# Attention two's scores as three rounded products, with the od modulation dealt out anew

## The chip, the cores and the metric

The kernel runs on one core of a Trainium2 chip. The metric is the device time of one execution in microseconds (us), and the time of a kernel is the median of its runs. The engines are TensorE (PE in the rows, PEld its weight loads), VectorE (DVE), ScalarE (ACT), GpSimd (POOL) and SyncE (SP). Each works through its own queue in order, and they meet on semaphores. SyncE and GpSimd here mainly issue DMAs.

## The reference, cut to what matters

Two transformer blocks on x of 256 tokens by 2048 features. The first has causal attention with 8 heads, a conformer convolution and a feed-forward of width 8192. The second has an attention layer ("ev") and a pooling layer ("od"), both with modulation vectors, which are a product of silu(c) with a 2048 x 6144 matrix each:

```
def _modulation(cvec, w, b):
    m = jax.nn.silu(cvec) @ w + b              # shift, scale, gate
...
h  = _rmsnorm(x, pre_g) * (1 + scale) + shift
hc = _rmsnorm(ctx, pre_g) * (1 + scale_c) + shift_c
qA, qB = _split_q(proj[..., :Q_W])             # 8 + 8 heads of 128
kA, vA, kB, vB = _split_kv(...)                # 2 + 2 heads of 128, of x and of ctx
outA = _dense_attention(rope(norm(qA)), [rope(norm(kA)), norm(kA_c)], [vA, vA_c])
outB = _window_attention(rope(qB), rope(kB), vB, kB_c, vB_c, sink)
y = jnp.concatenate([outA, outB], axis=-1) * jax.nn.silu(z)
x = x + gate * _rmsnorm(y @ w_out, post_g)
```

So the second attention has 16 query heads over 256 tokens, each against 512 keys (256 of x, 256 of the context); four query heads share one key head. Everything is float32.

## The kernel before, in words

Products with weights are taken in three rounded parts: a float32 operand is split into a high part, rounded to the type fp32r, and a low part (the rest), and hi x hi, hi x lo and lo x hi are summed. Weights come in blocks of 2048 x 512, by SyncE, a quarter at a time into `raw` (four quarters). A block has 8 steps of 256 rows. Per step ScalarE writes `w_hi` from `raw` (`split_hi`, L552), VectorE writes `w_lo` = raw - w_hi (`split_lo`, L1152), and TensorE multiplies. `w_hi` and `w_lo` have four slots, so ScalarE can split step s+4 once TensorE is done with step s (`step_done`). A quarter of `raw` is loaded again when VectorE is done with it (`split_done`).

Between these splits VectorE does the modulation: `mod_step` (L1192) multiplies 128x1024 of the modulation matrix by a column of silu(c) and adds it to `mod_sum`. Such a multiply-add is called a piece or a half; a vector such as od_shift or od_scale has 32 of them, numbered from 0. The first two (L1189) are plain multiplies. GpSimd loads each piece into one of two halves of `mod_raw` (`load_half`), once the piece two before it is done. After a vector, `turn_parts` transposes and reduces its sum. Where pieces stand is written out by hand. In the feed-forward `ff_mods` counts places p = 8 x block + i (32 blocks of 8 places) and deals pieces out with `spread`; od_shift begins at p = 209, which is in the last group (blocks 24 to 31: four hidden blocks that fill `b_hi`/`b_lo` with relu squared, then four outer ones). In block 28 and on VectorE also adds the block's product to the sum (`last_add`, L1725), ScalarE takes its squares, and VectorE multiplies by the gain and forms products with x (L1736, L1541). SyncE loads two other tensors, `grow` and `table`, once the last hidden part is ready (`hid_ready`, set by `hidden_low`, L1670), and the weights of block 29 and on stand behind them in its queue.

The second attention's projections follow: `evq` (4 blocks, queries), `evkv` (2 blocks, keys and values, each step for x and for the context, so twice as long), `evz` (4 blocks, z). Queries and keys are normed and roped on VectorE, transposed on TensorE and copied out by ScalarE (`q_out`) to `q_T` and `k_T`. While queries are done, the context's columns are scaled, rounded and split in pairs (`ctx_scale`, `ctx_pair`, `ctx_low`).

The heads run beside the z blocks, in 16 slots h = 4i + j (`head_slots` on each engine). TensorE in slot h: scores of head h (L2462), first half of the transposes of head h-1's probabilities (L2437), a z step, the other half, another z step, then v weighed with head h-1's probabilities (L2446). GpSimd stages each query in `q_stage2` and, at every fourth head, v in `v_stage2`. VectorE: maximum (L1874), `late_rope` in slot 0 alone, the normalizing (L1892), two splits, two od_scale pieces. ScalarE: copy of head h-2's output (L990), copy of the first transposed half (L985), exponentials (L1016), a split, the copy of the other half, a split; in slots 4, 8 and 12 first the silu of a z block (L997), which TensorE needs before its first z step of that slot. In slot 2 the keys of the last eight heads are transposed and copied out too.

## Time and profile before

| | |
|---|---|
| median of 3 runs | 1817.17 us (1816.78 to 1817.61) |
| the profiled execution | 1817.8 us, its span 1816.1 us |
| TensorE busy | 1795.7 us (99%) |
| VectorE busy | 1472.4 us (81%) |
| ScalarE busy | 903.3 us (50%) |
| granted TensorE clock | 0.999 |
| DMA | 429.02 MB, 236 GB/s over the span |

TensorE's rows overlap, since matmuls are pipelined: the time that a matmul holds the engine is the distance between two starts, not the length of the row. The same holds to a small part on VectorE and ScalarE, where the next instruction starts up to 0.1 us before the row of the one ahead ends.

### The profile page before, as it was taken

Reading aid. Unit: us, or ns where it says so; the run is one execution under the profiler, and the core shown is the slowest. Engines: PE = TensorE matmul, PEld = TensorE weight load, DVE = VectorE, ACT = ScalarE, POOL = GpSimd, SP = SyncE. Lnnn points to the kernel's source line nnn. Section 1 sums busy time; section 2 is a strip of 40 time slices with the busy share of each in tenths; the row PEclk is TensorE's granted clock in tenths of the full one; section 3 lists DMA queues with packets and bytes.
Section 4 is the critical chain, followed back from the end, with each engine's and each line's share of the span. In section 5 each row is a group of like instructions: output and inputs, shape, how many; then the busy total and the mean of one; then the engine's idle time right before and its main releaser. Section 6 shows DMA issues by size and latency. Waiting matters only on the chain.

```text
span 1816.1 us, 26040 instructions
## 1 busy us (share of the span) xinstructions
PE 1795.7 (99%) x9838; PEld 1553.2 (86%) x9838; DVE 1472.4 (81%) x1712; ACT 903.3 (50%) x1176; POOL 113.5 (6%) x217
## 2 busy tenths in 40 slices
PE   8999999999999999999999999999999999999998
PEld 7899988888888888888888888888888888888986
DVE  6899998878888897889887878765788778897854
ACT  6444566555434433543354557523566546445443
POOL 0000000000000000000000000011111000001000
PEclk9999999999999999999999999999999999999999
DMA  9756447777786787778977966565665784878563
GB/s 324 256 179 192 157 162 291 268 242 265 257 291 228 257 289 233 244 259 295 246 250 267 315 233 235 191 209 164 214 219 191 285 291 130 282 239 283 191 220 105
DMA packets 191304, 429.02 MB, mean 236 GB/s; under 512 B 12512, under 2 KB 12896, under 8 KB 189792
## 3 DMA queue, kind: packets, MB, share of 16 engines
q1 hardware_dynamic: 158560, 323.74, 52.6%
q0 software_dynamic: 27648, 100.68, 16.8%
q10 hardware_dynamic: 4992, 3.16, 0.6%
q8 instruction: 72, 1.18, 0.3%
q14 instruction: 32, 0.26, 0.0%
HBM read 423.33 MB, written 4.21 MB: 235 GB/s over the span
## 4 chain that ended last, share of the span: by engine, by line
PE 94%; DVE 3%; DMA 2%; ACT 1%; issue 1%; SPq 0%; DVEq 0%; ACTq 0%
PE banks L2090 23%; PE banks L2135 14%; PE banks L2137 14%; PE banks L2136 14%; PE banks L2096 12%; PE banks L2081 3%; PE banks L2083 3%; PE banks L2082 3%; PE banks L2446 2%; PE banks L2462 2%; PE banks L2199 1%; PE banks L2437 1%; DVE w_lo L1152 1%; DMA gate_rows<-mod_cols 1%; DMA raw<-in_od_w_out 0%
## 5 line engine op out<-in xcount | busy, mean ns | idle before, releaser
L552 ACT ACTIVATE w_hi<-raw 128x1024 fp32r<-128x1024 f32 x552 | 579.2, 1058 | 648.0 <-PE banks L2137 322.5
L1152 DVE TENSOR_TENSOR w_lo<-raw,w_hi 128x1024 fp32r<-128x1024 f32 x552 | 666.6, 1221 | 229.2 <-ACT w_hi L552 227.0
L2090 PE MATMUL banks<-a_pair,w_hi 128*128 128x512 f32 x1792 | 431.2, 391 | 1.6 <-DVE a_pair L1254 0.9
L2090 PEld LDWEIGHTS banks<-a_pair,w_hi 128*128 128x128 f32 x1792 | 328.4, 188 | 65.2 <-issue 2.2
L2135 PE MATMUL banks<-w_hi,b_hi 128*128 128x512 f32 x808 | 316.2, 391 | 0.2 <-DVE b_lo L1425 0.2
L2137 PE MATMUL banks<-w_hi,b_lo 128*128 128x512 f32 x808 | 314.5, 389 | 0.0
L1192 DVE SCALAR_TENSOR_TENSOR mod_sum<-mod_raw,silu_c,mod_sum 128x1024 f32<-128x1024 f32 x240 | 302.7, 1283 | 14.4 <-DMA mod_raw<-in_od_mod_w 8.1
L2136 PE MATMUL banks<-w_lo,b_hi 128*128 128x512 f32 x808 | 314.4, 389 | 0.0
L2096 PEld LDWEIGHTS banks<-a_pair,w_lo 128*128 128x128 f32 x1792 | 230.2, 191 | 8.8
L2096 PE MATMUL banks<-a_pair,w_lo 128*128 128x256 f32 x1792 | 234.6, 283 | 0.0
L2135 PEld LDWEIGHTS banks<-w_hi,b_hi 128*128 128x128 f32 x808 | 151.7, 188 | 31.9 <-DVE b_lo L1425 0.6
L2137 PEld LDWEIGHTS banks<-w_hi,b_lo 128*128 128x128 f32 x808 | 151.7, 188 | 31.6
L2136 PEld LDWEIGHTS banks<-w_lo,b_hi 128*128 128x128 f32 x808 | 151.7, 188 | 31.3
L2081 PE MATMUL banks<-a_pair,w_hi 128*128 128x256 f32 x512 | 148.4, 290 | 0.0
L2135 PE MATMUL banks<-w_hi,a_pair 128*128 128x512 f32 x368 | 145.1, 394 | 2.0 <-DVE a_pair L1282 0.7
L2083 PE MATMUL banks<-a_pair,w_lo 128*128 128x256 f32 x512 | 144.8, 283 | 0.0
L2082 PE MATMUL banks<-a_pair,w_hi 128*128 128x256 f32 x512 | 144.8, 283 | 0.0
L2137 PE MATMUL banks<-w_hi,a_pair 128*128 128x512 f32 x368 | 143.3, 389 | 0.0
L2136 PE MATMUL banks<-w_lo,a_pair 128*128 128x512 f32 x368 | 143.3, 389 | 0.0
L1368 DVE SCALAR_TENSOR_TENSOR mod_sum<-scratch,cols,mod_sum 128x256 f32<-128x256 f32 x240 | 98.8, 477 | 0.0
L2082 PEld LDWEIGHTS banks<-a_pair,w_hi 128*128 128x128 f32 x512 | 98.2, 192 | 0.3 <-issue 0.2
L2081 PEld LDWEIGHTS banks<-a_pair,w_hi 128*128 128x128 f32 x512 | 98.2, 192 | 0.4 <-ACT scratch L974 0.3
(249 smaller groups left out, 1679.3 us busy)
## 6 DMA issues: line engine op xcount, KB each, us to landing
raw<-in_w_ff SPq DMA_DIRECT2D x128, 1024.0 KB, 6.7
mod_raw<-in_ev_mod_w POOLq DMA_DIRECT2D x96, 512.0 KB, 5.2
mod_raw<-in_od_mod_w POOLq DMA_DIRECT2D x96, 512.0 KB, 5.7
raw<-in_ev_w_in SPq DMA_DIRECT2D x40, 1024.0 KB, 5.7
raw<-in_w_in SPq DMA_DIRECT2D x39, 1024.0 KB, 5.1
raw<-in_od_w_in SPq DMA_DIRECT2D x32, 1024.0 KB, 6.7
raw<-in_w_out SPq DMA_DIRECT2D x16, 1024.0 KB, 6.3
raw<-in_ev_w_out SPq DMA_DIRECT2D x16, 1024.0 KB, 6.8
```

Of the source, the lines that this page charges most:

```text
L552: nc.scalar.activation(w_hi[:, s % SLOTS], raw[:, s // 2, KPS * (s % 2):KPS * (s % 2) + KPS, :], ACT.Copy).then_inc(hi_ready, 1)
L1152: nc.vector.tensor_tensor(w_lo[:, s % SLOTS], raw[:, s // 2, KPS * (s % 2):KPS * (s % 2) + KPS, :], w_hi[:, s % SLOTS].bitcast(F32), ALU.s ...
L1192: nc.vector.scalar_tensor_tensor(s, mod_raw[:, half, :], c, s, ALU.mult, ALU.add).then_inc(mod_acc, 1)
L1368: e = nc.vector.scalar_tensor_tensor(y, src, w, y, ALU.mult, ALU.add)
L2081: nc.tensor.matmul(o, wh, hi[:, k, :], start=first and t == 0 and f % 2 == 0, stop=False, skip_group_check=True)
L2082: nc.tensor.matmul(o, wh, lo[:, k, :], start=False, stop=False, skip_group_check=True)
L2083: last = nc.tensor.matmul(o, wl, hi[:, k, :], start=False, stop=t == KPS - 1, skip_group_check=True)
L2090: e = nc.tensor.matmul(out[:, f, :], w_hi[:, s % SLOTS, t, P * f:P * (f + 1)], rows[:, :, KPS * s + t, :], start=s == 0 and t == 0, stop=F ...
L2096: e = nc.tensor.matmul(out[:, f, T:2 * T], w_lo[:, s % SLOTS, t, P * f:P * (f + 1)], rows[:, 0, KPS * s + t, :], start=False, stop=s == ST ...
L2135: nc.tensor.matmul(o, ah, w_hi[:, slot, t, :], start=s == 0 and t == 0, stop=False, skip_group_check=True)
L2136: nc.tensor.matmul(o, ah, w_lo[:, slot, t, :], start=False, stop=False, skip_group_check=True)
L2137: last = nc.tensor.matmul(o, lo[:, k, P * tt:P * (tt + 1)], w_hi[:, slot, t, :], skip_group_check=True, start=False, stop=s == STEPS - 1 a ...
```

## The change

- The scores of attention two are taken in three rounded products. ScalarE writes the keys rounded (`k_hi`, in `b_hi`) instead of `k_T`, and rounds each query (`round_q`), two heads ahead; VectorE forms the low parts (`keys_low`, `query_low`, into `b_lo`). GpSimd's query copies go.
- ScalarE copies the other half of the transposed probabilities ahead of its split instead of behind it.
- od_shift has 28 of its pieces in the feed-forward, in the place of 16, one in the queries, and three in the first key block, where it is now also turned. od_scale begins there: piece 0 in the first key block, 1 to 8 in the second, two a slot in heads 0 to 7 and one a slot in heads 8 to 14.
- In the last round of the queries the three context pairs stand one place earlier.
- The loops over heads are written out on TensorE, VectorE and in part ScalarE.

```
-            k_T = view(R1, 4, 512)
+            k_hi = [b_hi[:, 4 * i + 2:4 * i + 4, :] for i in range(4)]
+            k_lo = [b_lo[:, 4 * i + 2:4 * i + 4, :] for i in range(4)]
...
GpSimd, heads
-            pool.wait_ge(q_T_ready, 5)
-            stage_q(0, 0)
             first_loads("od_scale", "od", 1, "od_shift")
+            load_mod("od_scale", "od", 1, 1, 5)
+            load_half("od_scale", "od", 1, 5, 0)
+            for h in range(15):
+                if h % 4 == 0:
+                    pool.wait_ge(pv_done, HEAD2 + h + 2)
+                    nc.gpsimd.tensor_copy(v_stage2, v_tok2[:, :, span(h // 4 * HD, HD)]).then_inc(v_staged, 1)
+                for piece in (range(11 + 2 * h, 13 + 2 * h) if h < 8 else range(h + 19, h + 20) if h < 13 else ()):
+                    load_half("od_scale", "od", 1, piece // 2, piece % 2)
...
ScalarE
+            def round_q(h, tile):
+                nc.scalar.activation(b_hi[:, span(tile, 1), :], q_T[:, span(h, 1), :], ACT.Copy).then_inc(q_rounded, 1)
...
                     e.then_inc(exp_done, 1)
+                    if not first or j >= 1:
+                        prob_copy(h - 1, 1)
+                    if j < 2 or not last:
+                        round_q(h + 2, 4 * (i + j // 2) + j % 2)
                     split_hi(ahead[0], [ahead[1]])
                     if first and j == 2:
                         q_out(5)
-                    if not first or j >= 1:
-                        prob_copy(h - 1, 1)
...
VectorE
-                        halves("od_shift", *spread(p, 209, 246, 16))
+                        halves("od_shift", *spread(p, 209, 246, 28))
...
+            def keys_beside(i):
+                if i < 3:
+                    halves("od_shift", 29 + i, 1)
+                elif i < 7:
+                    turn_parts("od_shift", 0, 0, 3, raw_temp, i - 3, 1)
+                else:
+                    halves("od_scale", 0, 1)
...
+            def keys_low(m):
+                dve.wait_ge(q_T_ready, 5 + m)
+                ...
+                e.then_inc(k_low, 1)
+
+            def query_low(h, tile):
+                dve.wait_ge(q_rounded, h + 1)
+                nc.vector.tensor_tensor(b_lo[:, span(tile, 1), :], q_T[:, span(h, 1), :], b_hi[:, span(tile, 1), :].bitcast(F32),
+                                        ALU.subtract).then_inc(q_staged, 1)
...
             def last_keys_beside(i):
+                if i == 4:
+                    keys_low(0)
+                    query_low(0, 0)
+                    query_low(1, 1)
+                halves("od_scale", 1 + i, 1)
...
+                    if first and j == 2:
+                        keys_low(1)
                     split_lo(ahead[0], [ahead[1]])
-                    mod_step("od_scale", 4 * i + j, 0)
+                    if h < 14:
+                        query_low(h + 2, 4 * (i + j // 2) + j % 2)
+                    if h < 15:
+                        halves("od_scale", 2 * h + 9 if h < 8 else h + 17, 1)
                     if j == 3 and not first:
                         z_split(i - 1)
                     split_lo(ahead[0], [ahead[1] + 1])
-                    mod_step("od_scale", 4 * i + j, 1)
+                    if h < 8:
+                        halves("od_scale", 2 * h + 10, 1)
...
TensorE
-                    if first and j in (1, 3):
+                    if first and j in (0, 3):
+                        pe.wait_ge(k_low, 1 + j // 3)
+                    if first and j == 1:
                         pe.wait_ge(acc_free, 2 + ACC["evz"])
-                        pe.wait_ge(q_T_ready, 6 if j == 3 else 5)
                     pe.wait_ge(q_staged, h + 1)
                     for tt in range(TT):
-                        e = nc.tensor.matmul(score2[j % 2][:, 512 * tt:512 * (tt + 1)], q_stage2[:, j % 2, P * tt:P * (tt + 1)],
-                                             k_T[:, span(i, 1), :].rearrange("p a t -> p (a t)"), start=True, stop=True)
+                        out = score2[j % 2][:, 512 * tt:512 * (tt + 1)]
+                        qh = b_hi[:, 4 * i + j % 2, P * tt:P * (tt + 1)]
+                        nc.tensor.matmul(out, qh, k_hi[i].rearrange("p a t -> p (a t)"), start=True, stop=False)
+                        nc.tensor.matmul(out, qh, k_lo[i].rearrange("p a t -> p (a t)"), start=False, stop=False)
+                        e = nc.tensor.matmul(out, b_lo[:, 4 * i + j % 2, P * tt:P * (tt + 1)], k_hi[i].rearrange("p a t -> p (a t)"),
+                                             start=False, stop=True)
```

ScalarE's queue in the slots of heads 1 and 2, before (L552 is a split, L1016 the exponentials, L985 a copy of transposed probabilities, L990 of a head's output, L926 of the keys):

```order
355 L1016 ACTIVATE mod_sum,soft<-banks,soft 128x512 x2
356 L552 ACTIVATE w_hi<-raw 128x1024
357 L985 ACTIVATE scratch<-banks 128x512
358 L552 ACTIVATE w_hi<-raw 128x1024
359 L990 ACTIVATE scratch<-banks 128x256
360 L985 ACTIVATE scratch<-banks 128x512
361 L1016 ACTIVATE mod_sum,soft<-banks,soft 128x512 x2
362 L552 ACTIVATE w_hi<-raw 128x1024
363 L926 ACTIVATE scratch<-banks 128x1024
364 L985 ACTIVATE scratch<-banks 128x512
365 L552 ACTIVATE w_hi<-raw 128x1024
```

And after (L543 is the split, L1020 the exponentials, L989 the probability copy, L926 the rounding of a query, L921 the rounding of the keys):

```order
357 L1020 ACTIVATE mod_sum,soft<-banks,soft 128x512 x2
358 L989 ACTIVATE scratch<-banks 128x512
359 L926 ACTIVATE b_hi<-scratch 128x256
360 L543 ACTIVATE w_hi<-raw 128x1024 x2
361 L994 ACTIVATE scratch<-banks 128x256
362 L989 ACTIVATE scratch<-banks 128x512
363 L1020 ACTIVATE mod_sum,soft<-banks,soft 128x512 x2
364 L989 ACTIVATE scratch<-banks 128x512
365 L926 ACTIVATE b_hi<-scratch 128x256
366 L543 ACTIVATE w_hi<-raw 128x1024
367 L921 ACTIVATE b_hi<-banks 128x512 x2
368 L543 ACTIVATE w_hi<-raw 128x1024
```

The copy of the other half moved from behind the first split to ahead of it, with a rounding between them, and the keys' copy of slot 2 is two copies, now the last thing before the second split.

VectorE's queue from the last split of the key blocks to the reduce of head 1, before (L1874 is the maximum, L1790 to L1795 `late_rope`, L1189 a first piece):

```order
725 L1152 TENSOR_TENSOR w_lo<-raw,w_hi 128x1024
726 L1874 TENSOR_REDUCE soft<-banks 128x2
727 L1880 TENSOR_SCALAR soft<-soft 128x2
...
733 L1892 TENSOR_SCALAR mod_sum<-mod_sum,soft 128x512 x2
734 L1152 TENSOR_TENSOR w_lo<-raw,w_hi 128x1024
735 L1189 TENSOR_SCALAR mod_sum<-mod_raw,silu_c 128x1024
736 L1152 TENSOR_TENSOR w_lo<-raw,w_hi 128x1024
737 L1189 TENSOR_SCALAR mod_sum<-mod_raw,silu_c 128x1024
738 L1874 TENSOR_REDUCE soft<-banks 128x2
```

And after (L1158 is the split, L1198 a piece, L1907 the maximum, L1866 a query's low part):

```order
747 L1158 TENSOR_TENSOR w_lo<-raw,w_hi 128x1024
748 L1198 SCALAR_TENSOR_TENSOR mod_sum<-mod_raw,silu_c,mod_sum 128x1024
749 L1907 TENSOR_REDUCE soft<-banks 128x2
750 L1913 TENSOR_SCALAR soft<-soft 128x2
...
756 L1925 TENSOR_SCALAR mod_sum<-mod_sum,soft 128x512 x2
757 L1158 TENSOR_TENSOR w_lo<-raw,w_hi 128x1024
758 L1866 TENSOR_TENSOR b_lo<-scratch,b_hi 128x256
759 L1198 SCALAR_TENSOR_TENSOR mod_sum<-mod_raw,silu_c,mod_sum 128x1024
760 L1158 TENSOR_TENSOR w_lo<-raw,w_hi 128x1024
761 L1198 SCALAR_TENSOR_TENSOR mod_sum<-mod_raw,silu_c,mod_sum 128x1024
762 L1907 TENSOR_REDUCE soft<-banks 128x2
```

A piece stands ahead of the first maximum, the two of slot 0 are of the longer form, and a subtract is new.

VectorE in the feed-forward, from `hidden_low` of the last hidden block (L1670) to the first `last_add` (L1725), before:

```order
538 L1670 TENSOR_TENSOR b_lo<-scratch,b_hi 128x1024
539 L1152 TENSOR_TENSOR w_lo<-raw,w_hi 128x1024
540 L1192 SCALAR_TENSOR_TENSOR mod_sum<-mod_raw,silu_c,mod_sum 128x1024
541 L1152 TENSOR_TENSOR w_lo<-raw,w_hi 128x1024 x2
542 L1192 SCALAR_TENSOR_TENSOR mod_sum<-mod_raw,silu_c,mod_sum 128x1024
543 L1152 TENSOR_TENSOR w_lo<-raw,w_hi 128x1024 x2
544 L1192 SCALAR_TENSOR_TENSOR mod_sum<-mod_raw,silu_c,mod_sum 128x1024
545 L1152 TENSOR_TENSOR w_lo<-raw,w_hi 128x1024 x2
546 L1725 TENSOR_TENSOR scratch<-scratch,banks 128x512 x2
```

And after, from L1676 to L1731:

```order
546 L1676 TENSOR_TENSOR b_lo<-scratch,b_hi 128x1024
547 L1198 SCALAR_TENSOR_TENSOR mod_sum<-mod_raw,silu_c,mod_sum 128x1024
548 L1158 TENSOR_TENSOR w_lo<-raw,w_hi 128x1024 x2
549 L1198 SCALAR_TENSOR_TENSOR mod_sum<-mod_raw,silu_c,mod_sum 128x1024
550 L1158 TENSOR_TENSOR w_lo<-raw,w_hi 128x1024
551 L1198 SCALAR_TENSOR_TENSOR mod_sum<-mod_raw,silu_c,mod_sum 128x1024
552 L1158 TENSOR_TENSOR w_lo<-raw,w_hi 128x1024
553 L1198 SCALAR_TENSOR_TENSOR mod_sum<-mod_raw,silu_c,mod_sum 128x1024
554 L1158 TENSOR_TENSOR w_lo<-raw,w_hi 128x1024 x2
555 L1198 SCALAR_TENSOR_TENSOR mod_sum<-mod_raw,silu_c,mod_sum 128x1024
556 L1158 TENSOR_TENSOR w_lo<-raw,w_hi 128x1024
557 L1198 SCALAR_TENSOR_TENSOR mod_sum<-mod_raw,silu_c,mod_sum 128x1024
558 L1731 TENSOR_TENSOR scratch<-scratch,banks 128x512 x2
```

Six pieces stand there in the place of three, among the same seven splits.

## Rows read from the trace of the kernel before

**Rows 1.** The page: busy time, share of the span, instructions.
```profile
PE 1795.7 (99%) x9838; PEld 1553.2 (86%) x9838; DVE 1472.4 (81%) x1712; ACT 903.3 (50%) x1176; POOL 113.5 (6%) x217
```

**Rows 2.** Timeline of PE, end of keys, slot 1: start, us, engine, line, op, count.
```profile
1253.37 0.39 PE L2135 MATMUL banks<-w_hi,b_hi 128*128 128x512 f32 x1
...
1255.86 0.39 PE L2137 MATMUL banks<-w_hi,b_lo 128*128 128x512 f32 x1
...
1263.55 1.88 PE L2462 MATMUL banks<-scratch 128*128 128x512 f32 x4
1265.26 0.60 PE L2437 MATMUL banks<-ident,mod_sum 128*128 128x128 f32 x4
...
1268.58 0.60 PE L2437 MATMUL banks<-ident,mod_sum 128*128 128x128 f32 x4
...
1273.64 1.88 PE L2462 MATMUL banks<-scratch 128*128 128x512 f32 x4
```

**Rows 3.** Timeline of DVE, slots 0 and 1.
```profile
1263.81 1.22 DVE L1152 TENSOR_TENSOR w_lo<-raw,w_hi 128x1024 fp32r<-128x1024 f32 x1
1264.94 0.74 DVE L1189 TENSOR_SCALAR mod_sum<-mod_raw,silu_c 128x1024 f32<-128x1024 f32 x1
...
1267.40 1.22 DVE L1874 TENSOR_REDUCE soft<-banks 128x2 f32<-128x1024 f32 x1
```

**Rows 4.** Timeline of ACT, slot 1: in brackets idle time before, and what ended it.
```profile
1268.85 0.69 ACT L1016 ACTIVATE mod_sum<-banks,soft 128x512 f32<-128x512 f32 x1 [2.36 <-DVE soft L1880]
...
1270.19 1.05 ACT L552 ACTIVATE w_hi<-raw 128x1024 fp32r<-128x1024 f32 x1
1271.14 0.59 ACT L985 ACTIVATE scratch<-banks 128x512 f32<-128x512 f32 x1
```

**Rows 5.** Timeline of DVE and ACT, slot 6: a reduce and its exponentials.
```profile
1316.72 1.23 DVE L1874 TENSOR_REDUCE soft<-banks 128x2 f32<-128x1024 f32 x1
...
1318.43 0.69 ACT L1016 ACTIVATE mod_sum<-banks,soft 128x512 f32<-128x512 f32 x1 [0.68 <-DVE soft L1880]
```

**Rows 6.** Groups by line: busy us, mean ns, idle before and releasers.
```profile
L990 ACT ACTIVATE scratch<-banks 128x256 f32<-128x256 f32 (+1 forms) x16 | 6.1, 383 | 8.6 <-PE banks L2446 8.6
L1476 DVE TENSOR_TENSOR b_lo<-scratch,b_hi 128x256 fp32r<-128x256 f32 x8 | 3.2, 422 | 0.4 <-ACT b_hi L793 0.4
```

**Rows 7.** Timeline of ACT, slot 4: the silu of a z block.
```profile
1294.20 1.28 ACT L997 ACT_TABLE_LOAD   x1
1295.50 1.02 ACT L997 ACTIVATE scratch<-banks 128x1024 f32<-128x1024 f32 x1
```

**Rows 8.** Timeline of ACT, feed-forward, last group.
```profile
985.78 1.06 ACT L552 ACTIVATE w_hi<-raw 128x1024 fp32r<-128x1024 f32 x1 [1.66 <-PE banks L2137]
993.24 2.01 ACT L552 ACTIVATE w_hi<-raw 128x1024 fp32r<-128x1024 f32 x2 [6.39 <-DMA raw<-in_w_ff]
```

**Rows 9.** Timeline of DVE, feed-forward, last group.
```profile
982.84 1.22 DVE L1152 TENSOR_TENSOR w_lo<-raw,w_hi 128x1024 fp32r<-128x1024 f32 x1
...
994.33 2.36 DVE L1152 TENSOR_TENSOR w_lo<-raw,w_hi 128x1024 fp32r<-128x1024 f32 x2 [5.03 <-ACT w_hi L552]
...
1000.53 1.28 DVE L1725 TENSOR_TENSOR scratch<-scratch,banks 128x512 f32<-128x512 f32 x2
1003.57 1.22 DVE L1152 TENSOR_TENSOR w_lo<-raw,w_hi 128x1024 fp32r<-128x1024 f32 x1 [1.75 <-ACT w_hi L552]
```

**Rows 10.** Timeline of DVE, around 335 us: pieces close together.
```profile
333.08 1.28 DVE L1192 SCALAR_TENSOR_TENSOR mod_sum<-mod_raw,silu_c,mod_sum 128x1024 f32<-128x1024 f32 x1
334.28 1.21 DVE L1406 TENSOR_TENSOR w_lo<-raw,w_hi 128x1024 fp32r<-128x1024 f32 x1
...
336.84 1.28 DVE L1192 SCALAR_TENSOR_TENSOR mod_sum<-mod_raw,silu_c,mod_sum 128x1024 f32<-128x1024 f32 x1 [1.35 <-DMA mod_raw<-in_ev_mod_w]
...
340.02 1.28 DVE L1192 SCALAR_TENSOR_TENSOR mod_sum<-mod_raw,silu_c,mod_sum 128x1024 f32<-128x1024 f32 x1 [0.76 <-DMA mod_raw<-in_ev_mod_w]
```

**Rows 11.** Waits of PE, 1060 to 1250 us: total, times, longest.
```profile
PE banks L2135 <- DVE b_lo L1323: 0.6, 1, 0.6
```

More of the change, by code:

```diff
@@ L519, in _ @@
             load_mod("od_shift", "od", 0, 1, KT)
-            def stage_q(h, par):
-                if not isinstance(h, int) or h >= 2:
-                    pool.wait_ge(scores, HEAD2 + h - 1)
-                nc.gpsimd.tensor_copy(q_stage2[:, par, :], q_T[:, span(h, 1), :].rearrange("p a t -> p (a t)")).then_inc(q_staged, 1)
-            def head_slots(i, slots):
-                for j in slots:
-                    stage_q(4 * i + j + 1, (j + 1) % 2)
-                    if j == 0:
-                        pool.wait_ge(pv_done, HEAD2 + 4 * i + 2)
-                        nc.gpsimd.tensor_copy(v_stage2, v_tok2[:, :, span(i * HD, HD)]).then_inc(v_staged, 1)
-                    for half in range(2):
-                        load_half("od_scale", "od", 1, 4 * i + j + 1, half)
-            pool.wait_ge(q_T_ready, 5)
-            stage_q(0, 0)
-            first_loads("od_scale", "od", 1, "od_shift")
-            with pool.Fori(0, 3) as i:
-                head_slots(i, range(4))
-            head_slots(3, range(3))
+            first_loads("od_scale", "od", 1, "od_shift")
+            load_mod("od_scale", "od", 1, 1, 5)
[6 more added lines that the diff above has]
+                    load_half("od_scale", "od", 1, piece // 2, piece % 2)
             first_loads("od_gate", "od", 2, "od_scale")
@@ L949, in _ @@
                     q_out(n - 1)
[L950 to L951 removed]
+                split_hi(b + 1, (5, 6))
+                if n == 2:
+                    ctx_pair(pairs[0])
+                split_hi(b + 1, [7])
+                ctx_pair(pairs[n // 2])
                 split_hi(b + 2, (0, 1))
[L953 removed]
+                ctx_pair(pairs[1 + n // 2])
                 split_hi(b + 2, [2])
[L955 removed]
+                if n == 1:
                     ctx_pair(pairs[2])
@@ L1001, in z_round, with head_slots @@
                 nc.scalar.activation(b_hi[:, span(4 * i, FT), :], q_T[:, span(4 * i, FT), :], ACT.Copy).then_inc(z_hi, 1)
-            def head_slots(i, windowed, first=False):
+            def head_slots(i, windowed, first=False, last=False):
                 for j in range(4):
@@ L1032, in _ @@
             head_slots(1, False)
-            with act.Fori(2, 4) as i:
-                head_slots(i, True)
+            head_slots(2, True)
+            head_slots(3, True, last=True)
             prob_copy(15, 0)
@@ L1898, in head_slots @@
                     split_lo(ahead[0], [ahead[1] + 1])
-                    mod_step("od_scale", 4 * i + j, 1)
+                    if h < 8:
+                        halves("od_scale", 2 * h + 10, 1)
             head_slots(0, False, True)
             head_slots(1, False)
-            with dve.Fori(2, 4) as i:
+            for i in range(2, 4):
                 head_slots(i, True)
@@ L2479, in _ @@
             head_slots(0, True)
-            with pe.Fori(1, 4) as i:
+            for i in range(1, 4):
                 head_slots(i)
```

45 lines of the change are left out of this document (25 added, 20 removed).

## The prediction

> **What bounds the kernel now.** I read the busy table of the page first: TensorE is busy 1795.7 of 1816.1 us [rows 1], so only what shortens its own work, or makes it wait, can move the time. Then I read its timeline through the second attention. Each head there is one "slot" on TensorE: the scores, four transposes, a step of the z product (24 rounded matmuls), four transposes, another such step, and the product with v. Slot 1 runs from 1263.55 to 1273.64, 10.09 us, with nothing missing between the parts [rows 2]. VectorE and ScalarE serve it from behind: the softmax, and the splitting of raw weights into w_hi (ScalarE) and w_lo (VectorE), some steps ahead. VectorE also works through the modulation in "pieces", one 128x1024 multiply-add each, for which it waits for nobody as a rule. So the question is what the change takes from TensorE, and whether the two helpers keep their lead with the work dealt out anew.
>
> **What TensorE saves.** A head's scores are two products of 128x512, and they hold TensorE from 1263.55 to 1265.26, 1.71 us [rows 2]. The new form is six rounded matmuls of 512 columns with the pattern of the weight products; twelve of those start between 1253.37 and 1255.86 (eleven intervals), 0.226 us each [rows 2]. Six are 1.36 us. Saved: 0.35 x 16 heads = 5.7 us. The end of the q blocks gets one context pair earlier, which can take away the one wait of 0.6 us that stands there [rows 11]. With nothing else the kernel would stand at 1817.8 - 6.3 = 1811.5 by its own profiled execution.
>
> **What the attention gives back.** I follow the slots with the intervals of the rows: split 1.13 (1263.81 to 1264.94) [rows 3], piece 1.20 (333.08 to 334.28) [rows 10], reduce to exponentials 1.45 [rows 3, 4] or 1.71 [rows 5], exponentials 1.34 and probability copy about 0.5 [rows 4]. The new rounding of a query on ScalarE has the size of its 128x256 copies, 0.38 [rows 6], of which about 0.1 overlaps its neighbour (estimate, as piece and split overlap); the new subtract on VectorE is that of a 128x256 row, 0.42 [rows 6], 0.36 without overlap. Bounds for both: not below 0.2 and not above the 0.5 to 0.6 of the 128x512 copy [rows 4]; the chosen values are those of rows of the same size.
> Slot 0 and 1. Before, the last key block ended on a split, and slot 0 had the two first pieces, plain multiplies of 0.74, 0.66 without overlap [rows 3]. Now piece 8 stands ahead of the first reduce (+1.20), slot 0 has two full pieces (+1.1) and a query subtract (+0.36). Head 0's probabilities, ready by 1263.81 [rows 3], come at 1265.0; TensorE, 0.35 earlier than before, asks at 1263.55 - 0.35 + 1.36 = 1264.55: a wait of 0.5. The reduce of head 1 goes from 1267.40 to 1270.05. Behind it in ScalarE's queue are the exponentials and only then the second copy of head 0's probabilities, which ends at 1270.05 + 1.45 + 1.34 + 0.5 = 1273.4. Before, that copy ended at 1271.73 [rows 4] and TensorE used it at 1268.58 + 3.31 = 1271.89 [rows 2]: no room at all. Now it asks at 1271.7: a wait of 1.7.
> Slots 2 and 3. VectorE now must subtract the keys of heads 8 to 15 before TensorE may start scores 3, and ScalarE writes their rounded form only after exponentials, copy, rounding and a split. After the copy at 1273.4 ScalarE rounds and splits till 1274.7, VectorE then does split, subtract, piece, split, piece (5.0) and begins the reduce of head 2 at 1279.75: 1279.8 + 1.45 + 1.34 + 0.5 + 0.3 + 1.0 + 1.0 (two key copies) = 1285.4, subtract 1.25, so 1286.65. TensorE began slot 2 at 1275.2 and with the key transposes (0.87) needs 10.6 for it, so it asks at 1285.8: 1.0 of wait, and 0.65 more at v, since VectorE comes late to head 3.
> From slot 3 on a loop closes: ScalarE's split stands behind copy and rounding, and VectorE's rest of the slot behind that split. 1.71 + 1.34 + 0.5 + 0.3 + 1.05 = 4.9, then split 1.14, subtract 0.36, piece, split, piece (3.54): 9.9 us a slot against TensorE's 9.73. VectorE doesn't regain its lead in heads 3 to 7. In heads 8 to 14 one piece is gone but the band's add is there: 9.6, just enough. So at each head 4, 8 and 12 the z-silu, with its table load, comes late. Before, it ran from 1295.50 to about 1296.5 [rows 7] for a TensorE that needs it some 2.07 us into the slot (1265.26 + 0.36 after 1263.55), 0.2 later. Now TensorE asks 0.35 earlier and ScalarE is about a microsecond later: 1.1, 0.8, 0.9, and 1.1 at v in slot 8, behind the z_split of VectorE (1.14). Sum of waits 7.7, less 5.7 saved: the attention ends about 2.0 us later than before. With 1.45 in all slots it is +1.1, with 1.71 in all +2.9; the outer ends are -5.7 (no wait) and about +6 (each wait half as large again). The other moves of this stretch I put at nothing: GpSimd's query copies go, its four v copies now wait for a v product with two loads queued behind each, but such a load is wanted some 8 us after that product and loads took 5 to 6.9 in pairs [rows 10]; the first key block loses VectorE work while TensorE waits for nothing there; the unrolled loops hold the same instructions. Bounds 0 and 0.5 each.
> The Trainium skill (ScalarE: Activation LUTs, What ACT_TABLE_LOAD costs) counts 1.28 us for the load and 1.38 more of drain at each switch. Here the load starts at 1294.20 and the silu at 1295.50 [rows 7], so only the 1.28 shows, and I use that; by the page each of the three heads would be 1.4 later still, which by an estimate is +4.
>
> **What the feed-forward gives.** Between places 209 and 246 (944 to about 1043 us) 28 pieces stand where 16 stood: 12 x 1.20 = 14.4 us more on VectorE, and their loads. Nobody on TensorE waits in this stretch before. Two things make it tight. First the loads: mod_raw has two buffers, so piece n+2 is loaded only once n is done. Where pieces follow each other closely, starts two apart are 6.94 us apart (333.08 to 340.02, with VectorE waiting 0.76 for the DMA [rows 10]): 3.5 us a piece at best. 28 pieces in 37 places are 3.6 us a piece on average, but they stand three in a row at 2.7, so most triples wait 1 to 2 us, in VectorE's queue, ahead of splits and of hidden_low.
> Second the entry to the last outer blocks. SP holds the weights of the second outer block behind two other loads, and these behind hidden_low, which ends at 982.84 + a little (the row of that start is the split behind it [rows 9]). ScalarE waited 6.39 us for these weights, till 993.24, and the split on VectorE started at 994.33 [rows 8, 9] and was done at 995.5. TensorE needs it at 985.6 (step 3 done [rows 8]) + 4 x 2.72 = 996.5. So 1.0 us of room. Now one piece (1.20) and a wait of 1 to 1.5 come ahead of hidden_low: everything moves 2.5 us, a wait of about 1.7. Then, up to the add that ends the block (1000.53 before), there are three pieces for one, the start is 2.5 later, one more load wait of 1.5: about 1007. The add releases ScalarE's squares and then the split of step 4, which on VectorE starts 3.04 later (1003.57 - 1000.53 [rows 9]): 1010.1, done 1011.3, against a need at 996.5 + 1.7 + 4 x 2.72 = 1009.1: 2.3 more. Each of the two blocks after that costs VectorE 8 x 1.13 + 6 x 1.20 + 2.6 (gained and products) + 1.3 (add) + 1.75 (idle behind the add [rows 9]) = 21.9 and about a microsecond of load waits, against 21.8 of TensorE: about 1.2 each. Sum +6.4. If two pieces need 6.0 us instead of 6.9, the same count gives +1.7 to +4; if they need 8, as they may when the weights catch up after 984, +10 to +13. Bounds 0 and 14.
>
> **Sum.** 1817.8 + 2.0 + 6.4 - 0.6 = 1825.6; the median of the runs is 0.6 below the profiled one, so 1825.0.
>
> **Rivals.**
> 1. The saving arrives. VectorE is busy only 81% [rows 1], and the waits above are each about a microsecond, at the edge. If rounding and reordering cost nothing visible: 1817.2 - 5.7 - 0.6, with 0 to 1 from the feed-forward: 1811 to 1812. Against it: the margins of 0.2 us at the v product and the silu in slots 1 and 4 [rows 2, 4, 7]. Chance 0.15.
> 2. The feed-forward hides its pieces (loads land within 4.5 us there), the attention goes as worked out: 1817.2 + 2.0 - 0.6 + 1 = about 1819.6, no change that can be told. Chance 0.2.
> 3. The loads get slower under 28 pieces, so VectorE is late throughout: +12 instead of +6.4, 1831. For it: the loads of this stretch compete with 1 MB of weights each 5.4 us. Chance 0.12.
> 4. The six products don't run at 0.226 but at the 0.43 of a pass of today's scores (1.71 / 4), since both operands change their source: 2.6 us a head, +0.9 x 16 = 14, 1831 to 1840. Against it: all weight products read b_hi as here [rows 2]. Chance 0.03.
> The forecast itself, 1821 to 1829, has 0.5.
>
> **How the numbers follow.** A difference under 0.2% (3.6 us) can't be told from none. Faster, below 1813.6: nearly all of rival 1, 0.15 with a little from elsewhere 0.16. Same, to 1820.8: rival 2 and the lower edge of the forecast, 0.25. Slower: 0.59. The range 1812.5 to 1832 leaves out half of rival 1 and the upper part of 3 and 4.
>
> **What would show it.** Right: the scores take 1.36 us a head; TensorE waits in slot 1 for a probability copy on ScalarE, in slot 3 for b_lo of the keys, in slots 4, 8 and 12 for the silu; VectorE's pieces wait for DMA between 950 and 1045; the first split of the second last outer block is later than 996.5, and TensorE waits for w_lo in three or four places there. Wrong: no TensorE wait between 940 and 1065, or slots of 9.7 us throughout, or a wait at a place where I have none, such as the first key block, where VectorE loses work.

## The result: 1830.0 us, slower by 0.7%

The changed kernel takes 1830.02 us (median of 6 runs, 1826.42 to 1831.24); the kernel before, run beside it, 1817.15 (1816.78 to 1818.3). The ratio is 1.0068, 95% interval 1.0055 to 1.0081. The profiled run of the changed kernel is its fastest, 1826.42 with a span of 1824.7: 8.6 over the span before. So its trace shows two thirds of the loss of the median.

The page of the changed kernel. TensorE is busy as long as in [rows 1], and the span is 8.6 longer:

```profile
span 1824.7 us, 25842 instructions
PE 1795.2 (98%) x9870; PEld 1560.7 (86%) x9870; DVE 1479.4 (81%) x1732; ACT 903.9 (50%) x1194; POOL 105.4 (6%) x201
```

What TensorE waited for, whole span (line and releaser: us in total, times, longest):

```profile
PE banks L2174 <- DVE w_lo L1158: 6.5, 4, 2.8
...
PE banks L2238 <- DVE ln_rstd L1252: 2.7, 2, 2.0
PE banks L2485 <- issue: 2.3, 2, 1.5
...
PE banks L2120 <- ACT scratch L1001: 0.7, 1, 0.7
PE banks L2504 <- DVE b_lo L1859: 0.6, 1, 0.6
PE banks L2476 <- DVE mod_sum L1925: 0.5, 1, 0.5
```

The first line is the feed-forward, the second the norm products behind it (the wait of 2.0 at 1077.14 was 1.15 before), the last four are the attention. To see what each stage costs, I lay TensorE's landmarks of both traces side by side (start of the same work, us):

| landmark | before | after | later by |
|---|---|---|---|
| end of the feed-forward's products (first `ones` product) | 1062.24 | 1071.19 | 8.95 |
| first norm product | 1067.35 | 1077.14 | 9.79 |
| scores of head 0 | 1256.09 | 1264.96 | 8.87 |
| v product of head 15 | 1422.23 | 1431.93 | 9.70 |
| end of the span | 1816.1 | 1824.7 | 8.6 |

So the feed-forward costs 8.95 and its tail 0.85 at the norm; the q blocks give back 0.9; the attention, whose slots are 5.2 shorter in all without their waits, loses 0.83; and 1.1 comes back behind it (0.6 of it a wait for w_lo at 1748 that the kernel before had and this one doesn't).

**The feed-forward.** TensorE's waits there:

```profile
999.14 0.47 PE L2174 MATMUL banks<-w_hi,b_hi 128*128 128x512 f32 x1 [2.75 <-DVE w_lo L1158]
...
1013.11 0.47 PE L2174 MATMUL banks<-w_hi,b_hi 128*128 128x512 f32 x1 [2.80 <-DVE w_lo L1158]
1013.42 0.40 PE L2175 MATMUL banks<-w_lo,b_hi 128*128 128x512 f32 x1
...
1014.74 0.63 PE L2174 MATMUL banks<-w_hi,b_hi 128*128 128x512 f32 x1
1015.17 0.63 PE L2175 MATMUL banks<-w_lo,b_hi 128*128 128x512 f32 x1
```

Two waits of 2.8 where the forecast had 1.7 and 2.3; two of 0.45 follow. Together 6.45, but the stage is 8.95 longer. The last two rows hold the rest: 1.6 us after the second wait the matmuls start every 0.43 us instead of every 0.23. The windows (busy time and count of PE, granted clock, DMA share, GB/s) say why:

```profile
1012.00:1016.00 4.00, 2.89 (x9) 0.79 0.70 274
1016.00:1020.00 4.00, 4.00 (x15) 0.78 0.63 186
1020.00:1024.00 4.00, 4.00 (x19) 1.00 1.04 406
```

The clock was at its lower level (1.2 GHz) for part of these eight microseconds. Eight matmuls, from 1014.33 on, start 0.43 apart in place of 0.23: 1.6 us more for the same work (1.7 by the windows, whose mean is 0.785). Each of the four waits costs 0.24 beyond its bracket, 1.0 in all: from 996.01, the last start ahead of the first wait, to 999.45, the second start behind it, are 3.44 us, where two intervals of 0.23 and the 2.75 make 3.20. Against that the outer blocks began 0.24 earlier than before (974.47 against 974.71).

Why w_lo was late shows on VectorE and ScalarE in the stretch of [rows 8, 9] (in brackets the idle time before and what ended it):

```profile
983.78 1.23 DVE L1676 TENSOR_TENSOR b_lo<-scratch,b_hi 128x1024 fp32r<-128x1024 f32 x1 [0.94 <-ACT b_hi L838]
...
994.27 1.28 DVE L1198 SCALAR_TENSOR_TENSOR mod_sum<-mod_raw,silu_c,mod_sum 128x1024 f32<-128x1024 f32 x1 [3.46 <-DMA mod_raw<-in_od_mod_w]
997.77 1.23 DVE L1158 TENSOR_TENSOR w_lo<-raw,w_hi 128x1024 fp32r<-128x1024 f32 x1 [2.22 <-ACT w_hi L543]
...
1007.51 1.28 DVE L1198 SCALAR_TENSOR_TENSOR mod_sum<-mod_raw,silu_c,mod_sum 128x1024 f32<-128x1024 f32 x1 [2.14 <-DMA mod_raw<-in_od_mod_w]
1008.71 1.28 DVE L1731 TENSOR_TENSOR scratch<-scratch,banks 128x512 f32<-128x512 f32 x2
1011.74 1.23 DVE L1158 TENSOR_TENSOR w_lo<-raw,w_hi 128x1024 fp32r<-128x1024 f32 x1 [1.75 <-ACT w_hi L543]
```

```profile
996.68 2.00 ACT L543 ACTIVATE w_hi<-raw 128x1024 fp32r<-128x1024 f32 x2 [10.07 <-DMA raw<-in_w_ff]
```

The weights of the second outer block come at 996.68 instead of 993.24, 3.4 later, and the first split starts at 997.77 instead of 994.33. Where the 3.4 us come from shows on SyncE's queue (start times, and the time from the first issue of these weights to ScalarE's first split of them):

| kernel | `hidden_low` | weights issued | first w_hi | issue to w_hi |
|---|---|---|---|---|
| before | 981.70 | 984.12 | 993.24 | 9.12 |
| changed | 983.78 | 986.21 | 996.68 | 10.47 |

So 2.1 us come from VectorE's queue ahead of `hidden_low`, and 1.35 from weights that take longer to land. The wait of 3.46 for the piece at 994.27 costs TensorE nothing by itself: the split behind it still waits 2.22 for the weights. The wait of 2.14 for the piece at 1007.51 does cost: it stands right ahead of the add. That add, forecast for "about 1007", begins at 1008.71, and the split of step 4 is at 1011.74, not 1010.1.

**The attention.** TensorE in slots 1 to 4, and ScalarE where it made TensorE wait:

```profile
1272.15 0.40 PE L2504 MATMUL banks<-b_hi 128*128 128x512 f32 x1
...
1274.16 0.66 PE L2476 MATMUL banks<-ident,mod_sum 128*128 128x128 f32 x4 [0.46 <-DVE mod_sum L1925]
...
1282.51 1.97 PE L2485 MATMUL banks<-scratch 128*128 128x256 f32 x8 [1.50 <-issue]
1284.12 0.59 PE L2504 MATMUL banks<-b_hi 128*128 128x512 f32 x1
...
1295.68 0.50 PE L2504 MATMUL banks<-b_hi 128*128 128x512 f32 x1 [0.60 <-DVE b_lo L1859]
...
1308.52 0.39 PE L2120 MATMUL banks<-a_pair,w_hi 128*128 128x256 f32 x1 [0.69 <-ACT scratch L1001]
```

```profile
1281.72 0.20 ACT L1020 ACTIVATION_READ_ACCUMULATOR mod_sum<-banks,soft 128x1 f32 x1
1281.81 0.59 ACT L989 ACTIVATE scratch<-banks 128x512 f32<-128x512 f32 x1
...
1306.14 1.28 ACT L1001 ACT_TABLE_LOAD   x1
1307.44 1.02 ACT L1001 ACTIVATE scratch<-banks 128x1024 f32<-128x1024 f32 x1
```

"issue" at 1282.51 is a wait that no semaphore record names; ScalarE's row at 1281.81 names it: the copy ends at 1282.40, and v starts 0.11 later. The places are those of the forecast: the probabilities and their second copy in slot 1, the keys' b_lo at scores 3, the silu at slot 4, and v in slot 8 (0.83); the silus of slots 8 and 12 delay their first z step by only 0.2 and 0.4. The slots of heads 0 to 14, from scores to scores, are 7.19, 11.97, 11.56, 9.97, 10.70, 9.74, 9.74, 9.74, 11.00, 9.87, 9.74, 9.74, 10.14, 9.77 and 9.74 us; without waits they are 9.74, and 10.61 for slot 2 with the key transposes. What is over is 2.23 + 0.95 + 0.23 + 0.96 + 1.26 + 0.13 + 0.43 = 6.2. Before, most slots took 10.07 or 10.08 (slot 1, with 10.09, is in [rows 2]), so 0.33 a head is saved.

### The profile page after: what moved, and what is told of

It reads as the page before. It is cut to its first block, busy times and chain, and to the rows that moved or that the text cites. A ratio compares the mean times of both kernels' runs of the same rounds, so it can differ in the third digit from the quotient of the medians.

```text
span 1824.7 us, 25842 instructions
## 1 busy us (share of the span) xinstructions
PE 1795.2 (98%) x9870; PEld 1560.7 (86%) x9870; DVE 1479.4 (81%) x1732; ACT 903.9 (50%) x1194; POOL 105.4 (6%) x201
## 3 DMA queue, kind: packets, MB, share of 16 engines
q8 instruction: 77, 1.26, 0.3%
## 4 chain that ended last, share of the span: by engine, by line
PE 80%; DVE 10%; DMA 4%; ACT 3%; issue 3%; DVEq 0%; POOLq 0%; ACTq 0%; SPq 0%
PE banks L2129 19%; PE banks L2174 13%; PE banks L2175 13%; PE banks L2176 13%; PE banks L2135 10%; DVE w_lo L1158 3%; DMA mod_raw<-in_od_mod_w 3%; PE banks L2120 2%; DVE mod_sum L1198 2%; PE banks L2122 2%; PE banks L2121 2%; PE banks L2238 1%; ACT w_hi L543 1%; DMA raw<-in_w_ff 1%; DVE soft L1907 1%
## 5 line engine op out<-in xcount | busy, mean ns | idle before, releaser
L543 ACT ACTIVATE w_hi<-raw 128x1024 fp32r<-128x1024 f32 x552 | 577.2, 1058 | 621.1 <-PE banks L2176 308.5
L1158 DVE TENSOR_TENSOR w_lo<-raw,w_hi 128x1024 fp32r<-128x1024 f32 x552 | 666.8, 1222 | 222.4 <-ACT w_hi L543 220.7
L1198 DVE SCALAR_TENSOR_TENSOR mod_sum<-mod_raw,silu_c,mod_sum 128x1024 f32<-128x1024 f32 x240 | 301.9, 1279 | 21.3 <-DMA mod_raw<-in_od_mod_w 14.4
```

The source lines that it names most:

```text
L543: nc.scalar.activation(w_hi[:, s % SLOTS], raw[:, s // 2, KPS * (s % 2):KPS * (s % 2) + KPS, :], ACT.Copy).then_inc(hi_ready, 1)
L1158: nc.vector.tensor_tensor(w_lo[:, s % SLOTS], raw[:, s // 2, KPS * (s % 2):KPS * (s % 2) + KPS, :], w_hi[:, s % SLOTS].bitcast(F32), ALU.s ...
L1198: nc.vector.scalar_tensor_tensor(s, mod_raw[:, half, :], c, s, ALU.mult, ALU.add).then_inc(mod_acc, 1)
```

## Experiments

All medians in us; the kernel before was run beside them each time, at 1817.1 to 1817.4. "Loads" is VectorE's idle time for mod_raw between 940 and 1062, and "FF" by how much later the first `ones` product starts than at 1062.24, both from the one profiled run.

| kernel | median | profiled | FF | loads |
|---|---|---|---|---|
| changed | 1830.0 | 1826.4 | 8.95 | 14.4 |
| feed-forward alone | 1830.9 | 1829.3 | 10.7 | 15.3 |
| scores alone | 1821.4 | 1821.2 | -0.2 | 0 |
| 24 pieces | 1821.5 | 1821.4 | 4.7 | 8.6 |
| 20 pieces | 1817.2 | 1816.9 | 0.25 | 1.0 |
| short loads | 1817.8 | 1817.8 | 1.2 | 3.2 |
| short pieces | 1821.0 | 1820.9 | 4.3 | 21.3 |
| copy first | 1828.3 | 1830.4 | 14.1 | 18.2 |
| best | 1810.7 | 1810.7 | 0.4 | 0.9 |

**1. The twelve pieces alone.**

```
 kernel before:
-   halves("od_shift", *spread(p, 209, 246, 16))
+   halves("od_shift", *spread(p, 209, 246, 28))
 (then piece 28 beside the last query block, 29 to 31 and the turn in the first key block)
```

> The kernel before with one part of the change: 28 pieces of the od modulation in the feed-forward instead of 16, the last four and the turn in the first key block; scores, slots and the od scale pieces as before. Theory 1 (the loss of the change is the twelve pieces in the feed-forward): the trace of the changed kernel loses 8.95 us between 975 and 1066 and 0.85 more at the first norm product behind it, so this kernel takes 1817.2 + 9 to 10 = 1826 to 1827, or up to 1831 if the median of the changed kernel is slower for the same cause. TensorE waits some 2.8 us for w_lo in two outer blocks and its granted clock falls behind the second. Rival (half of that loss comes with the shifted later stages or is chance of the profiled run): under 1822.

1830.89 (1828.23 to 1831.76), ratio 1.0073 (1.0059 to 1.0087): the whole loss of the change from this part. The profiled run has five waits for w_lo, 6.4 in all, but is 10.7 late at the end of the stage (0.8 of it was there before the outer blocks began); behind the first wait, of 2.77, the clock falls (windows as above), and it falls once more behind the norm products' wait of 2.00 at 1078.91 (0.94 and 0.63 in the windows from 1076 to 1084):

```profile
996.00:1000.00 4.00, 1.59 (x8) 1.00 1.02 382
1000.00:1004.00 4.00, 3.64 (x10) 0.63 1.05 404
1004.00:1008.00 4.00, 4.00 (x18) 0.95 1.04 394
```

**2. The scores alone.**

```
 changed kernel, with the dealing of before:
+   halves("od_shift", *spread(p, 209, 246, 16))   # 1, 11 and 4 behind it, as before
+   halves("od_scale", 2 * h, 1) ... halves("od_scale", 2 * h + 1, 1)   # in all 16 slots
```

> The changed kernel with the modulation dealt as in the kernel before: 16 pieces in the feed-forward, 11 in the first key block, 4 and the turn in the last, and two od scale pieces in each of the 16 slots. The three products and all roundings stay. Theory 1 (VectorE can't take rounded scores and two pieces in the band's slots): nothing lost in the feed-forward, slots 0 to 7 as in the changed kernel or a little better since no piece stands ahead of the first reduce, slots 8 to 15 at 10.4 to 10.6 us instead of 9.74, together 1817 to 1821. Rival (the slots hold at 9.74, since VectorE waits for others in each slot anyway): 1812 to 1815.

1821.42 (1821.17 to 1822.74), ratio 1.0023 (1.0014 to 1.0032). Nothing is lost in the feed-forward, and slot 1 takes 9.58: no piece stands ahead of the first reduce, and slot 0 has the two short first pieces again. But slots 9 to 14 take 11.07, 10.65, 10.66, 11.79, 11.07 and 10.66: two pieces beside the band's add are 0.9 too much for VectorE. So by themselves the new scores cost 4 us more than they save, and pieces had to leave these slots. Theory 1 held, with slots and time a little above its figures.

**3. 20 pieces, and 24.**

```
-   halves("od_shift", *spread(p, 209, 246, 28))
+   halves("od_shift", *spread(p, 209, 246, 20))   # or 24
 first key block, steps 0 to 5 (with 20 pieces; with 24 they are 7 pieces):
-   halves("od_shift", 29 + i, 1)                  # three steps
+   halves("od_shift", 21 + 2 * i, 2 if i < 5 else 1)
```

> The changed kernel with 20 pieces in the feed-forward instead of 28 and 11 in the first key block instead of 3, with the turn behind them there. Theory 1 (the feed-forward hides 20 pieces, since loads then have 4.9 us of places each; the first key block held 11 before): all 9.8 us of the feed-forward come back, 1816.6 by the profiled run of the changed kernel, up to 1820 by its median. Rival (the lateness at the entry of the last outer blocks had only 1.0 us of room and one more piece is enough): a third to a half comes back, 1822 to 1826. A second rival (the first key block becomes late): a new wait for w_lo between 1190 and 1240.

> As the changed kernel, but 24 pieces in the feed-forward and 7 in the first key block (the kernel with 20 and 11 took 1817.2 with no wait of TensorE in the feed-forward). Theory 1 (the two buffers' rate is the limit: places come every 2.7 us, 24 in 37 places leave 4.2 us a piece, above the 3.5 that two buffers need): the load waits mostly vanish, at most 1 us is lost, 1817 to 1818.5. Rival (there was 1.0 us of room at the entry of the last outer blocks, and each piece more than 16 takes its share of it): half the loss, 1821 to 1824.

20 pieces: 1817.20 (1816.74 to 1818.05), ratio 1.0000 (0.9991 to 1.0009). All 12.8 us between it and the changed kernel come from eight pieces in the feed-forward; no wait for w_lo is left there, and the first key block takes 11 without one. (Two later kernels with 20 pieces had one wait there, of 0.40 in experiment 6 and 0.27 in experiment 8: 20 is at the edge.) The slots are those of the changed kernel to 0.01. 24 pieces: 1821.49 (1820.41 to 1824.75), ratio 1.0024 (1.0014 to 1.0034), waits of 1.33, 2.14 and 0.64. Here my theory (24 fit, by their mean rate) was wrong and the rival right: the mean of 4.2 us a piece did not show it, since VectorE still waits 3.6 for one load (at 1022.06, shortly ahead of TensorE's wait of 2.14).

**4. Loads or VectorE's own time?**

```
 short loads (leaves out seven eighths of each od shift load):
-   nc.gpsimd.dma_start(mod_raw[:, half, :], ...)
+   nc.gpsimd.dma_start(mod_raw[:, half, 0:128], ...)
 short pieces (leaves out seven eighths of each od shift sum):
-   nc.vector.scalar_tensor_tensor(s, mod_raw[:, half, :], c, s, ...)
+   nc.vector.scalar_tensor_tensor(s[:, 0:128], mod_raw[:, half, 0:128], c, s[:, 0:128], ...)
```

> The changed kernel with 28 pieces in the feed-forward, each od shift piece computed over all 1024 columns but loaded for 128 of them only (an eighth of the bytes, the rest of the buffer stays as it was). Theory 1 (the loss is the loads' rate through two buffers and the waits it puts into VectorE's queue): VectorE waits for no load between 945 and 1050, TensorE loses under 1.5 us there, 1818 to 1820. Rival (VectorE's own 14.4 us for twelve more pieces is what makes it late): the losses at the two outer blocks stay above 4 us, 1824 or more.

> The changed kernel with full loads, but each od shift piece multiplies and adds only 128 of its 1024 columns, so it holds VectorE for about 0.25 us instead of 1.28. Theory 1 (loads' rate): each buffer is free a microsecond earlier, but the load waits at the entry of the last outer blocks stay (3.5 us at 994 in the changed kernel), 3 to 6 us of the 9.8 remain, 1821 to 1825. Rival (VectorE's own time): the loss goes, 1817 to 1819.

With short loads 1817.82 (1817.45 to 1818.8): 12.2 of the 12.8 come back while VectorE does all 28 pieces in full length; one wait of 0.67 is left. (VectorE does still wait for three loads, 3.2 in all: that part of the expectation was too round.) With short pieces 1821.02 (1819.81 to 1822.1): 9.0 of the 12.8 come back too, although every byte is loaded; 3.8 remain above the kernel with 20 pieces, with three waits for w_lo (3.34). VectorE even waits longer for loads:

```profile
991.90 0.35 DVE L1199 SCALAR_TENSOR_TENSOR mod_sum<-mod_raw,silu_c,mod_sum 128x128 f32<-128x128 f32 x1 [3.65 <-DMA mod_raw<-in_od_mod_w]
...
996.37 1.23 DVE L1158 TENSOR_TENSOR w_lo<-raw,w_hi 128x1024 fp32r<-128x1024 f32 x1 [4.12 <-ACT w_hi L543]
```

So neither side makes the loss alone. VectorE's time with hardly any bytes costs 0.6, the bytes with hardly any of VectorE's time cost 3.8, and the other 8.4 need both. (The 3.8 may be low for the bytes: a short piece also frees its buffer 0.9 us earlier.) The entry of the last outer blocks shows the two sides as in the table above:

| kernel | `hidden_low` | weights issued | first w_hi | issue to w_hi |
|---|---|---|---|---|
| short loads | 982.83 | 985.26 | 993.79 | 8.53 |
| short pieces | 982.11 | 984.53 | 995.28 | 10.75 |
| 20 pieces | 982.81 | 985.24 | 994.15 | 8.91 |

With short loads `hidden_low` is 1.1 late by VectorE's own pieces, and the weights land as fast as before. With short pieces it is only 0.4 late, and the weights take 1.6 longer. The changed kernel has both, and the waits of pieces for their loads on top.

**5. One copy moved.**

```
+   if first and j == 1: prob_copy(h - 1, 1)       # ahead of the exponentials, and no longer behind them
```

> The changed kernel with one ScalarE instruction moved in slot 1: the second copy of head 0's probabilities stands ahead of head 1's exponentials instead of behind them. The wait of 1.5 us at v in slot 1 goes. Theory 1 (that wait is a loss by itself): 1.5 us less than the changed kernel. Rival (VectorE's queue sets when head 2 is reduced and when the keys of heads 8 to 15 are subtracted, so TensorE only comes earlier to a wait that ends when it did): the wait at scores 3 grows from 0.6 to about 2.1 and the time stays within 0.3 us. I hold the rival for likelier.

1828.32 (1826.2 to 1830.35); the feed-forward's scatter hides a microsecond here, so I read the slots: slot 1 falls from 11.97 to 10.23, slot 2 rises from 11.56 to 12.82:

```profile
PE banks L2176 <- DVE w_lo L1160: 9.0, 5, 3.7
PE banks L2240 <- DVE ln_rstd L1254: 1.8, 2, 1.1
PE banks L2506 <- DVE b_lo L1861: 1.5, 1, 1.5
```

The wait for the keys is 1.5 instead of 0.6; of 1.74 us 0.5 stay. The rival held for 1.26 of them: VectorE's queue, not the copy, sets when slots 2 and 3 can go on. The first row belongs to the feed-forward: five waits, 9.0 us, two falls of the clock (0.70 to 0.87 in the windows), 14.1 us late.

**6. The silu between two splits** (with 20 pieces).

```
     split_hi(ahead[0], [ahead[1]])
+    if j == 3 and not last: z_silu(i)
     split_hi(ahead[0], [ahead[1] + 1])
-    if j == 0 and not first: z_silu(i - 1)        # was the next slot's first instruction
```

> The kernel with 20 pieces in the feed-forward, with the z-silu (and its table load) put between the two splits that end slots 3, 7 and 11 on ScalarE, instead of behind both. Theory 1 (the silu is late only because of the split ahead of it): the waits of 0.7 at slot 4 and of 0.8 at v in slot 8 go, and slot 12 falls from 10.14 to 9.74, about 1.5 to 2.5 us less than 1817.2. Rival (VectorE gets the second w_hi 2.3 us later and closes the loop 1 us later, so that the next slots wait instead): no gain, 1817 to 1818.

1817.74 (1817.29 to 1818.1) against 1817.20: no gain. The 15 slots together are 0.65 longer, and the feed-forward ends 0.6 later in this profiled run, which the move doesn't touch. Slot 4 fell from 10.70 to 10.29, slot 5 rose to 10.10 and slot 8 from 11.00 to 11.69 with 1.72 at v. VectorE gets its second w_hi later, as the rival said: its split of slot 3 comes 1.2 later (1299.57 against 1298.35, 0.6 of it the later start).

**7. The pieces dealt anew, without and with ScalarE's moves.**

```
 22 pieces in the feed-forward, 3 in the last query block, 7, the turn and four od scale
 pieces in the first key block, 8 in the last, none ahead of the first reduce;
 slots:
-   2 pieces in slots 0 to 7, 1 in 8 to 14
+   1 piece in slots 0 to 2, 2 in 3 to 7, 1 in 8 to 14
```

> As the changed kernel, but the pieces dealt anew: 22 in the feed-forward, 3 in the last query block, 7 and the turn and four od scale pieces in the first key block, 8 in the last with none ahead of the first reduce, one instead of two in slots 0 to 2. ScalarE's order is unchanged. Theory 1 (VectorE's queue sets slots 0 to 3): the reduces of heads 0 to 3 come 1.2 us or more earlier each, the wait for the probabilities in slot 1 (0.5), most of the 1.5 at v and the 0.6 at the keys go, 1817.2 - 3 = 1814 to 1815. Rival (the order on ScalarE sets them): slots 1 and 2 stay at 11.9 and 11.6 and the time at 1817.

> The dealing of the kernel above with three moves on ScalarE: the second copy of head 0's probabilities ahead of head 1's exponentials, the copies of the keys of heads 8 to 15 ahead of the rounding and the split of slot 2, and the silu between two splits. Theory 1 (all waits of the attention were these): the whole saving of the scores arrives, 1811.5 to 1813. Rival (the silu's new place costs VectorE what it gives): 1814 to 1815.

1815.47 (1814.1 to 1818.69) and 1816.38 (1813.86 to 1819.13); neither can be told from the kernel before (0.9995 and 0.9993), and the second missed its 1811.5 to 1813. The slots did what was expected: slot 1 from 11.97 to 9.55, slot 2 from 11.56 to 10.61, slot 3 from 9.97 to 9.74, in both kernels. ScalarE's order is unchanged in the first, so VectorE's queue alone made these waits. But 22 pieces in the feed-forward already cost 3.0 and 5.0 there; I had counted on nothing. In the second, a wait of 2.42 is followed by a window at 0.71:

```profile
1028.00:1032.00 4.00, 2.02 (x9) 1.00 0.79 271
1032.00:1036.00 4.00, 3.56 (x11) 0.71 0.18 27
1036.00:1040.00 4.00, 4.00 (x16) 0.87 1.01 377
```

**8. The best version, and the same without ScalarE's moves.**

```
 20 in the feed-forward, 4 in the last query block, 8 in the first key block;
 slots: 1 piece in 0 to 2 and in 7 to 15, 2 in 3 to 6
```

> The changed kernel with 20 pieces in the feed-forward (where 20 left no wait), 4 in the last query block, 8 and the turn and four od scale pieces in the first key block, 8 in the last, one in slots 0 to 2 and in slots 7 to 15, two in slots 3 to 6; on ScalarE the three moves of the kernel before it (probability copy, keys, silu). Theory 1: the feed-forward loses nothing, the slots hold as with 22 pieces, and the 0.9 left at slot 8 goes as slot 7 has one piece less: 1811 to 1812.5. Rival (the last query block or the first key block becomes late with one more piece each): a new wait between 1155 and 1245, 1814 to 1816.

> The same dealing of the pieces with ScalarE's order as in the changed kernel. Theory 1 (VectorE's queue alone set the slots): within 0.5 us of the kernel with the three moves. Rival (ScalarE's order matters once VectorE is early): 1 us or more slower, with waits at slots 4, 8 and 12 for the silu.

1810.68 (1810.12 to 1812.28), ratio 0.9965 (0.9951 to 0.9978), and 1811.10 (1810.91 to 1811.52), ratio 0.9966 (0.9952 to 0.9979). Every slot from 3 to 14 takes 9.74; without the moves slots 4, 8 and 12 take 9.93 or 9.94. Of the new waits of TensorE only the second row is left; the first was there before, and the kernel with ScalarE's order unchanged has not even the second:

```profile
PE banks L2244 <- DVE ln_rstd L1254: 1.8, 2, 1.1
...
PE banks L2180 <- DVE w_lo L1160: 0.3, 1, 0.3
```

1811.1 is 6.0 under the kernel before. The prediction's saving "with nothing else" was 6.3 (scores and q blocks), and nearly all of it arrives once both helpers keep up.

## Why the prediction was right, and where its sizes were off

The time was slower than before and in the range; the likeliest case said 1821 to 1829, the median is 1830.0, the profiled run 1826.4. By its terms:

- **Saved 5.7 by the scores:** slots are 0.33 shorter, slot 0 by 0.27, so 5.2 (the forecast's own 0.35 x 16 is 5.6). The six matmuls start 0.23 apart, as taken from the weight products. Rival 4 is out, and rival 1 with the time.
- **Saved 0.6 at the q blocks:** 0.9. The wait of 0.6 [rows 11] is gone in the changed kernel and in the scores alone, and stands in the feed-forward alone, which lacks the earlier pair.
- **Waits of the attention 7.7:** 6.2, at each place that was named. Slot 1 (0.5 + 1.7) came to 2.23, almost to the tenth. Slots 2 and 3 (1.65, where 1286.65 - 1285.8 is 0.85 and not 1.0) to 1.18. At the silus: 0.96 for 1.1 in slot 4, 1.39 in slots 8 and 9 for 0.8 and the 1.1 at v, 0.43 in slots 12 and 13 for 0.9. The loop of 9.9 us in heads 3 to 7 didn't reach TensorE: slots 5 to 7 hold at 9.74. VectorE's reduce of head 3 starts at 1300.54, that of head 6 at 1329.99, 9.82 apart in the mean: so it is there on VectorE, close to its 9.9, but TensorE doesn't wait for it (probably since the waits before had already made it late; no run parts that). The net of the attention is 0.8, not 2.0. Experiments 5 and 7 show the step behind it right: VectorE's queue is the cause, and ScalarE's copy is only where TensorE meets it.
- **The table load 1.28, not 1.38 more:** the silu starts 1.30 after the load [rows 7], and again here (1306.14 to 1307.44). The load of 1.28 is all that shows; the Trainium skill's further drain (ScalarE: Activation LUTs, What ACT_TABLE_LOAD costs) doesn't.
- **The feed-forward 6.4:** this is the term that was mis-sized. The waits of the profiled run are 6.45 in all, but that agreement is partly luck: 2.75 + 2.80 for 1.7 + 2.3, then 0.45 twice for 1.2 twice. The first is 1 us longer because the forecast let the weights land as fast as before, and they took 1.35 more; the 2.5 us by which everything was to move came to 2.1. And a wait was priced at its own length. It costs more: 2.5 in the profiled run (1.7 through the clock, 1.0 around the four waits, less the 0.24 of the earlier start), and 0.85 at the first norm product, where VectorE was still behind. That makes 9.8 for 6.4. In the median it is 12.8 (experiment 3), twice the forecast. The profiled runs of the two other kernels with 28 pieces, 10.7 and 14.1 late, show how such a stage scatters: five waits each, and two falls of the clock each up to the norm products. That the other five runs of the changed kernel are slower for the same reason is likely, but not shown: there is no trace of them.
- **Rival 3** (1831, loads slower under 28 pieces) ended nearest to the median, with my chance of 0.12. Its cause is not borne out over the stretch: from 940 to 1050 us a piece's load landed in 5.3 us (median), against 6.4 in the kernel before, and a weight load in 7.6 against 7.7. Only at the entry of the last outer blocks were the weights slower, by the 1.35 above.
- **Rival 2** (the feed-forward hides its pieces) is true of 20 pieces and false of 22.

Its signs came too, each in its place: 1.39 us of scores (6 x 0.23), the waits in slots 1, 3 and 4, pieces that wait for their loads, four waits for w_lo. The split that was to be later than 996.5 is that of the second outer block (the list of signs calls it the second last); it starts at 997.77. Unforeseen and small: 1.1 us came back behind the attention; of 0.5 of it the cause is open.

## What to carry to other kernels

Before moving work into a stage "with a free engine", count its bytes and its buffers beside the engine's time: here 14.4 us of VectorE work with hardly any bytes cost 0.6, and with their loads 12.8. A wait of TensorE costs more than its length where the clock falls behind it (here 1.7 us a fall, one or two falls in the profiled kernels with 28 full pieces), and where a stage has no slack its times scatter. When a wait names a late copy on one engine, look at what the queue of the other had ahead of it: moving the copy shifted the wait, taking pieces out of VectorE's queue removed it.
